# Loading the context in runs of 32 columns and turning it with VectorE's 32 by 32 block transposes

## What is computed

```
# reference, cut
x = first_block(...)          # mixers, gates, "mixed @ w_out", then an MLP: up, relu squared, down
hc = _modulate(_rmsnorm(ctx_2, norm_g), shift_c, scale_c)   # 256 x 2048
pc_kv = hc @ w_in_2[:, OFF_K:OFF_ZA]
kc = _rmsnorm(_heads(pc_kv, 0, 4), k_norm_g)
vc = _heads(pc_kv, KV_W, 4)
```

## Time and profile before

| | |
|---|---|
| median of 3 runs | 2193.26 us |
| the profiled execution, its own time | 2193.32 us |
| its span in the trace | 2191.5 us |
| TensorE busy (matmul) | 2180.9 us |
| TensorE weight load | 2050.2 us |
| VectorE busy | 1546.1 us (71%) |
| ScalarE busy | 1060.4 us (48%) |
| GpSimd busy | 103.1 us (5%) |
| DMA | 474.97 MB, mean 217 GB/s |

### The profile page before, as it was taken

How to read it: one execution, slowest core, us unless ns; L and a number is a source line. 1 busy time by engine, 2 the same in 40 slices (tenths; PEclk the granted TensorE clock), 3 DMA queues, 4 the chain that set the end, 5 groups by cost and what they waited for, 6 DMA issues and landing times.

```text
span 2191.5 us, 37576 instructions
## 1 busy us (share of the span) xinstructions
PE 2180.9 (100%) x15930; PEld 2050.2 (94%) x15930; DVE 1546.1 (71%) x1886; ACT 1060.4 (48%) x1382; POOL 103.1 (5%) x84
## 2 busy tenths in 40 slices
PE   9999999999999999999999999999999999999998
PEld 9999999999999889989988988998889999999987
DVE  7899588888889657544554555555768887776776
ACT  5444445544444546444543443444655555444443
POOL 1000000000000000000000000000101211110001
PEclk9999999999999999999999999999999999999999
DMA  8876676687787755656656656656755545678784
GB/s 276 245 242 199 199 252 223 227 279 259 253 282 263 240 183 182 194 192 193 195 194 194 194 194 196 200 191 204 246 172 164 165 136 178 220 269 285 257 276 158
DMA packets 248032, 474.97 MB, mean 217 GB/s; under 512 B 21526, under 2 KB 26000, under 8 KB 247096
## 3 DMA queue, kind: packets, MB, share of 16 engines
q1 hardware_dynamic: 243032, 454.40, 64.9%
q0 software_dynamic: 4832, 18.16, 2.5%
HBM read 468.30 MB, written 5.78 MB: 216 GB/s over the span
## 4 chain that ended last, share of the span: by engine, by line
PE 98%; DVE 1%; issue 0%; ACT 0%; DMA 0%; SPq 0%; DVEq 0%; POOLq 0%; POOL 0%; ACTq 0%
PE ps L907 21%; PE ps L909 20%; PE ps L908 20%; PE ps L900 11%; PE ps L901 11%; PE ps L902 11%; PE ps L825 1%; PE ps L703 0%; PE ps L748 0%; DMA raw<-in_w_in 0%; PE ps L735 0%; PE ps L814 0%; PE ps L813 0%; PE ps L815 0%; DVE wloW L1298 0%
## 5 line engine op out<-in xcount | busy, mean ns | idle before, releaser
L907 PE MATMUL ps<-op0h,whiW 128*128 128x256 f32 x3376 | 936.9, 278 | 1.4 <-DVE wloW L1298 1.2
L909 PE MATMUL ps<-op0h,wloW 128*128 128x256 f32 x3376 | 932.3, 276 | 0.0
L908 PE MATMUL ps<-op0l,whiW 128*128 128x256 f32 x3376 | 932.2, 276 | 0.0
L1298 DVE TENSOR_TENSOR wloW<-raw,whiW 128x1024 fp32r<-128x1024 f32 (+1 forms) x503 | 618.2, 1241 | 312.3 <-ACT whiW L954 310.3
L954 ACT ACTIVATE whiW<-raw 128x1024 fp32r<-128x1024 f32 (+1 forms) x504 | 529.7, 1059 | 574.6 <-PE ps L909 469.2
L907 PEld LDWEIGHTS ps<-op0h,whiW 128*128 128x128 f32 x3376 | 633.8, 188 | 4.0 <-DVE wloW L1298 2.1
L908 PEld LDWEIGHTS ps<-op0l,whiW 128*128 128x128 f32 x3376 | 633.9, 188 | 0.6
L909 PEld LDWEIGHTS ps<-op0h,wloW 128*128 128x128 f32 x3376 | 633.8, 188 | 0.0
L1298 DVE TENSOR_TENSOR wloT<-raw,whiT 128x1024 fp32r<-128x1024 f32 (+1 forms) x264 | 318.9, 1218 | 236.2 <-ACT whiT L954 235.0
L954 ACT ACTIVATE whiT<-raw 128x1024 fp32r<-128x1024 f32 (+1 forms) x264 | 273.9, 1048 | 286.2 <-PE ps L902 246.4
L900 PE MATMUL ps<-whiT,op1h 128*128 128x512 f32 x640 | 249.2, 389 | 0.0
(11 more groups left out here) (310 smaller groups left out, 2088.4 us busy)
## 6 DMA issues: line engine op xcount, KB each, us to landing
raw<-in_w_in SPq DMA_DIRECT2D x256, 512.0 KB, 4.3
raw<-in_w_up SPq DMA_DIRECT2D x128, 512.0 KB, 3.8
raw<-in_w_down SPq DMA_DIRECT2D x128, 512.0 KB, 4.0
raw<-in_w_ada SPq DMA_DIRECT2D x96, 512.0 KB, 4.5
raw<-in_w_gate SPq DMA_DIRECT2D x96, 512.0 KB, 5.0
raw<-in_w_out SPq DMA_DIRECT2D x64, 512.0 KB, 4.8
raw<-in_w_branch SPq DMA_DIRECT2D x48, 512.0 KB, 5.0
raw<-in_w_proj_a SPq DMA_DIRECT2D x24, 512.0 KB, 5.0
```

Source lines behind the costliest of these rows:

```text
L907: pe.matmul(o, wh, xh[:, ka, :], start=first and m % 2 == 0, stop=False, skip_group_check=True)
L908: pe.matmul(o, wh, xl[:, ka, :], start=False, stop=False, skip_group_check=True)
L909: mm = pe.matmul(o, wl, xh[:, ka, :], start=False, stop=last, skip_group_check=True)
L1298: v.tensor_tensor(wlo[job.mode][q % NSPL][:, :, 0:job.n], x, h.bitcast(F32), ALU.subtract).then_inc(s_lo, 1)
```

## The change

The context is loaded in another layout, and the turn from tokens on partitions to channels on partitions is done by VectorE.

- The load: 32 DMAs of 64 KB on GpSimd's queue instead of 4 of 512 KB, all behind one wait for the end of `g23` and all counted on one semaphore (512). Each brings 32 tokens (b) of 32 of every 128 channels (g) to 32 partitions: 16 runs of 32 columns, 128 bytes each, per partition. Partition 32g + r then holds token 32b + r, channels 128k + 32g to 128k + 32g + 31.
- The sums: `ctx_square` now stands in steps 272 and 273 and is four activations each, one for a group of 32 tokens, into eight columns. The sum of one token is spread over four partitions, so TensorE adds them in step 274 with a new part `ctx_sums`, one product of `foldm` with the eight columns. VectorE's `ctx_var` (step 275) adds eps to all eight, GpSimd takes the power once instead of twice, and `ctx_norm` (steps 276 and 277) is four instructions of 128x512 each.
- The turn: `ctx_turn(i)`, i = 0 to 7, on VectorE in step 278 + i is one transpose of 128x512 in 32 by 32 blocks from `ctxs` to `ctxt`, both on SBUF. The 32 products with the identity are gone from TensorE. ScalarE's `turn_x` for the unit stands in the same step 278 + i and reads `ctxt`, VectorE's stands in step 279 + i, ahead of `ctx_turn(i + 1)` in the table.

```diff
@@ -225,10 +225,9 @@
         for tt in range(2):
-            q = of["wo0"].first + 3 + 2 * tt
+            q = of["wo2"].first + tt
             side(act_at, q, "ctx_square", tt)
-            side(dve_at, q, "row_var", 1, tt)
-            side(dve_at, q + 1, "row_norm", 1, tt)
+            side(dve_at, q + 4, "ctx_norm", tt)
             q = of["wo3"].end + 1 + tt
@@ -239,7 +238,14 @@
             side(dve_at, q + 1, "row_norm", 3, tt)
-        for s, q0, n in ((1, of["wo0"].first + 9, 1), (2, of["kc"].first + 6, 2), (3, of["vc"].first + 7, 2)):
+        side(pe_at, of["wo2"].first + 2, "ctx_sums")
+        side(dve_at, of["wo2"].first + 3, "ctx_var")
+        for i in range(8):
+            q = of["wo2"].first + 6 + i
+            side(dve_at, q, "ctx_turn", i)
+            side(act_at, q, "turn_x", 8 + i)
+            side(dve_at, q + 1, "turn_x", 8 + i)
+        for s, q0, n in ((2, of["kc"].first + 6, 2), (3, of["vc"].first + 7, 2)):
             for i in range(8):
...
@@ -370,8 +376,8 @@
         g1b = bg("g1b", [128, 2048], 0)
-        ctxs = at("ctxs", [128, 2, 2048], op0_at)
-        ctxj = at("ctxj", [128, 2048], op0_at + 16384)
+        ctxs = at("ctxs", [128, 16, 8, 32], op0_at)
+        ctxt = at("ctxt", [128, 16, 256], op0_at + 16384)
         zs = bg("zs", [128, 16, 256], 8)
...
@@ -478,7 +484,7 @@
-            w = 4 if name in QK else 1
+            w = 8 if name == "ctx" else 4 if name in QK else 1
             c = col(f"n_{name}{tt}", 2 * w)
@@ -592,12 +598,12 @@
                 pool.dma_start(X[:, t, c:c + 1024], a["x"][0, 128 * t:128 * t + 128, c:c + 1024]).then_inc(s_xr, 16)
-            for i in range(4):
-                t, c = i // 2, 1024 * (i % 2)
-                pool.wait_ge(s_pe, of["g23"].end + 2 * i)
-                pool.dma_start(ctxs[:, t, c:c + 1024], a["ctx_2"][0, 128 * t:128 * t + 128, c:c + 1024]).then_inc(s_ctxin[t], 16)
+            ctx_parts = a["ctx_2"][0].rearrange("(b r) (k g c) -> g b r k c", r=32, g=4, c=32)
+            pool.wait_ge(s_pe, of["g23"].end)
+            for g in range(4):
+                for b in range(8):
+                    pool.dma_start(ctxs[32 * g:32 * g + 32, :, b, :], ctx_parts[g, b]).then_inc(s_ctxin, 16)
             rstd("ctx", 0)
-            rstd("ctx", 1)
             rstd("mixed", 0)
@@ -685,15 +691,12 @@
                     return
-                src = (None, ctxs, macc, macc)[s]
+                src = macc
                 ps = bank[4 + u % 4]
...
                     pe.wait_ge(s_turned, u - 11)
-                elif kp == 0 and s == 1:
-                    pe.wait_ge(s_ya, 8)
-                    pe.wait_ge(s_acol, 1)
                 elif s == 2:
@@ -712,6 +715,11 @@
                 pe.matmul(bank[4][0:8, 0:384], a5[0:32, 0:8], oneh[0:32, :], start=True, stop=True).then_inc(s_erow, 1)
+
+            def ctx_sums():
+                pe.wait_ge(s_sumsq, 4)
+                pe.wait_ge(s_ya, 8)
+                pe.matmul(bank[5][:, 0:8], foldm[:, :], norm_col("ctx", 0)[0], start=True, stop=True).then_inc(s_ctxsum, 1)
...
@@ -957,10 +965,11 @@
             def ctx_square(tt):
-                act.wait_ge(s_ctxin[tt], 32)
-                if tt:
-                    act.wait_ge(s_sumsq, 3)
-                square(ctxs, ctxj[:, :], "ctx", tt)
+                act.wait_ge(s_ctxin, 512)
+                for b in range(4 * tt, 4 * tt + 4):
+                    junk = ctxt[:, 2 * b:2 * b + 2, :].rearrange("p k (b c) -> p (k b) c", c=32)
+                    op = act.activation(junk, ctxs[:, :, b, :], ACT.Square, accum_out=norm_col("ctx", 0)[0][:, b:b + 1])
+                op.then_inc(s_sumsq, 1)
@@ -981,6 +990,8 @@
                 ps, tm = bank[4 + u % 4], tmp[2 + u % 2]
+                if s == 1:
+                    ps = ctxt[:, 2 * kp:2 * kp + 2, :].rearrange("p k t -> p (k t)")
                 act.wait_ge(s_turn, u - 7)
@@ -1333,6 +1344,24 @@
+            def ctx_var():
+                ss, rs = norm_col("ctx", 0)
+                v.wait_ge(s_ctxsum, 1)
+                v.tensor_scalar(rs, bank[5][:, 0:8], 1.0 / D, EPS, ALU.mult, ALU.add).then_inc(s_var, 1)
+
+            def ctx_norm(tt):
+                v.wait_ge(s_rstd, norm_no["ctx", 0])
+                for b in range(4 * tt, 4 * tt + 4):
+                    x = ctxs[:, :, b, :]
+                    op = v.tensor_scalar(x, x, norm_col("ctx", 0)[1][:, b:b + 1], None, ALU.mult)
+                op.then_inc(s_rows, 1)
+
+            def ctx_turn(i):
+                k = slice(2 * i, 2 * i + 2)
+                if i == 0:
+                    v.wait_ge(s_rows, 2)
+                v.transpose(ctxt[:, k, :].rearrange("p k t -> p (k t)"), ctxs[:, k, :, :].rearrange("p k b c -> p (k b c)")).then_inc(s_turn, 1)
+
             def row_var(s, tt):
```

More of the change, by code:

```diff
@@ L330, in program @@
         gqk = sb("gqk", [128, 2, 128])
-        mhalf = sb("mhalf", [128, 4])
+        mhalf = sb("mhalf", [128, 8])
         recip = sb("recip", [128, 16])
@@ L448, in program @@
         s_brm, s_mixv, s_mixh, s_mix = sem("branch_summed"), sem("mix_value"), sem("mix_high"), sem("mix_operand")
-        s_ctxin, s_xr, s_g1b = [sem("ctx_rows0"), sem("ctx_rows1")], sem("x_again"), sem("g1b")
+        s_ctxin, s_ctxsum, s_xr, s_g1b = sem("ctx_rows"), sem("ctx_sums"), sem("x_again"), sem("g1b")
         s_wosq, s_x1 = sem("wout_square"), sem("x1_rows")
@@ L468, in program @@
         s_out = [sem(f"out{i}") for i in range(5)]
-        norms = [("x0", 0), ("x0", 1), ("ctx", 0), ("ctx", 1), ("mixed", 0), ("mixed", 1), ("x1", 0), ("x1", 1), ("kc", 0), ("kc", 1),
+        norms = [("x0", 0), ("x0", 1), ("ctx", 0), ("mixed", 0), ("mixed", 1), ("x1", 0), ("x1", 1), ("kc", 0), ("kc", 1),
                  ("mlp", 0), ("mlp", 1), ("x2", 0), ("x2", 1), ("k", 0), ("k", 1), ("qq0", 0), ("qq0", 1), ("qq1", 0), ("qq1", 1),
@@ L847, in fourier_d @@
                 mm.then_inc(s_fd, 1)
-            parts = {"turn_x": turn_x, "vectors_b": vectors_b, "bias_row": bias_row, "ada_fold": ada_fold, "index_dots": index_dots, "pool_weight": pool_weight,
+            parts = {"turn_x": turn_x, "vectors_b": vectors_b, "bias_row": bias_row, "ctx_sums": ctx_sums, "ada_fold": ada_fold, "index_dots": index_dots, "pool_weight": pool_weight,
                      "scores1": scores1, "turn1": turn1, "values1": values1, "turn_x": turn_x,
@@ L1638, in _ @@
                      "softmax1_max": softmax1_max, "softmax1_scale": softmax1_scale, "values1": values1, "fold_map": fold_map, "ada_quarters": ada_quarters,
-                     "ada_columns": ada_columns, "row_var": row_var, "row_norm": row_norm, "turn_x": turn_x, "x1_add": x1_add, "mlp_add": mlp_add,
+                     "ada_columns": ada_columns, "ctx_var": ctx_var, "ctx_norm": ctx_norm, "ctx_turn": ctx_turn, "row_var": row_var, "row_norm": row_norm, "turn_x": turn_x, "x1_add": x1_add, "mlp_add": mlp_add,
                      "turn_qk": turn_qk, "split_kc": split_kc, "rotate": rotate, "softmax2_max": softmax2_max, "softmax2_less": softmax2_less, "softmax2_sum": softmax2_sum,
```

## The result

The changed kernel takes 2208.38 us, the median of 6 runs (2207.72 to 2209.63); the kernel before took 2193.27 us beside it (6 runs, 2193.2 to 2193.96). The ratio is 1.0069, 95% interval [1.0059, 1.008]: 15 us slower. The profiled execution took 2208.33 us, its span 2206.5 us, 15.0 more than the span before.

What follows compares the result with a forecast made beforehand. TensorE, busy end to end and 98% of the chain that ended last, was taken to bound the kernel. The sum was 2193.3 - 3.5 + 2.0 + 12.8 + 1.9 = 2206.5 us, 0.6% slower, range 2201.5 to 2215.

Steps and rivals of the forecast that it cites:

- 1 identity products gone: TensorE's 32 products with the identity, two blocks of 16 at 1.75 us each, go: gain 3.50 us.
- 6 the load: The 32 small context loads on GpSimd's queue land 20 us and more before ScalarE wants them: no cost.
- 2 `ctx_sums`: TensorE waits 1.65 us for ScalarE's squares before `ctx_sums`, plus 0.35 for product and refilled pipeline: loss 2.0 us.
- 4 the rounds: Steps 278 to 285: ScalarE and VectorE wait for each other, 5.01 us a round against 2.72: loss 12.8 us.
- 5 after chunk 288: VectorE's backlog delays `x1_add`, making chunks 291 to 293 late: loss 1.9 us, between 0 and 4.
- The loop: Steps 278 to 285: ScalarE's and VectorE's parts form one circle of 5.01 us a round, costing 12.8 us.
- The wait at `ctx_sums`: TensorE, before `ctx_sums` in step 274, waits 1.65 us for both halves of ScalarE's squares; loss 2.0 us in all.
- rival C: TensorE's clock falls in the rounds, a chunk lasting 5.44 us: 5 to 8 us more, 2212 to 2215; chance 0.08.
- rival A: GpSimd's loads go one at a time, the last landing 43 us after ScalarE wants it: about 2250 us; chance 0.07.
- part 6: The context load: landing 737 to 752, wanted at 772, weights landing some microseconds later harmless; cost taken as nothing.
- Step 5: After chunk 288: `x1_add` starts some 5.5 us after it, chunks 291 to 293 come late: loss 1.9 us.
- Rival B: In steps 278 to 285 VectorE's and ScalarE's work overlaps, rounds costing nothing: 2191.8 us, within 0.2%; chance 0.08.

Runs made afterwards that it cites:

- e1: The changed kernel with ScalarE's and VectorE's `turn_x` of the context one step later: 2194.57 us, ratio 1.0004 to the kernel before.
- e3: The changed kernel with only the context's squares moved four steps earlier, to steps 268 and 269: 2205.57 us, ratio 1.0056 to the kernel before.
- e6: The changed kernel with one more block transpose of 128x512 ahead of each of the eight, into an unread PSUM bank: 2213.85 us, ratio 1.0094.
- e7: The changed kernel with four products on idle data put before each of chunks 284 to 288 on TensorE: 2209.84 us, ratio 1.0074.
- e5: The changed kernel with VectorE's block transpose of the next unit ahead of the cast and subtraction of the last: 2201.05 us, ratio 1.0042.
- e9: e1 with four products of 256 columns on idle data ahead of TensorE's wait in `ctx_sums`: 2193.00 us, ratio 1.0001 to the kernel before.
- e4: The kernel before with 32 loads in small runs into the old layout, the context's parts eight steps later: 2193.94 us, ratio 1.0003.
- e8: e2 with the 32 loads in four groups of eight, at the ends of chunks 252, 255, 258 and 261: 2190.84 us, ratio 0.9989.
- e2: e1 with the context's squares also moved from steps 272 and 273 to 268 and 269: 2191.03 us, ratio 0.9991 to the kernel before.

## Why the prediction was right, step by step

The start times on TensorE's timeline give each term apart. The distance to the first of x1's identity products (833.85 before, 848.31 after) is 14.46 us:

| Step | predicted | measured in the trace | from |
|---|---|---|---|
| 1 identity products gone | -3.50 | -3.49 | chunk 272 starts 3.32 us earlier (770.66 against 773.98), with 0.17 lost at 748 |
| 6 the load | 0 | +0.17 | gap before 748.81 |
| 2 `ctx_sums` | +2.0 | +2.16 | 775.87 to 778.26, less the 0.23 of a matmul |
| 4 the rounds | +12.8 | +13.2 | chunk 274 at 778.26 to 288 at 829.57, less 14 x 2.722 |
| 5 after chunk 288 | +1.9 | +2.39 | 18.74 against 16.35 us to x1's products |
| sum | +13.2 | +14.4 | |

Another 0.5 us lies behind it, in one place: at 1991.29 TensorE stands 0.55 us behind the matmul before it, where 0.11 is usual, because ScalarE had waited 4.4 us for raw weights of `w_in`. The kernel before, e1 and e3 have no such wait of TensorE there, and in three experiments with the same rounds (e3, e6, e7) the time behind x1's products is as long as before. So it belongs to this execution and not to the change. Every term of the forecast came out within 0.5 us, so the total is not luck. No miss took time off, and so 13.2 us were forecast and 15 measured.

**The loop** was the deciding step, and it held in each of its parts: 5.01 us forecast, 5.02 measured. Inside it two sizes were off and cancelled: ScalarE's two activations take 1.00 from SBUF where the earlier trace rows had 0.91 from PSUM, and the transpose with its hand-over 0.74 where 0.80 was assumed; from SBUF to SBUF it lasts 0.70, next to the row's 0.72. e1 (order alone changed, the rounds gone), e5 (one part taken out of the circle, 1.06 less per round) and e6 (one part doubled, 0.59 more per round) show the mechanism itself, not only its sum. The 0.4 us beyond the forecast is mainly lead: `ctx_norm` took 1.6 us a step where 1.45 was assumed, the first transpose started 18.4 us after chunk 272 instead of 18.0, and the lead at chunk 281 was 4.2 us instead of 4.4. (In its range, the terms of the low end add up to -5.2 and not to the -5.0 written; nothing hangs on it.)

**The wait at `ctx_sums`** was right in kind and size (1.76 us idle, 2.16 in all), but a consequence was missed: the clock. The prediction looked for a falling clock in the rounds only (rival C), and had a clock below 1.00 there as a sign of being wrong. That sign came, 0.89, and the price that C put on it, 5 to 8 us, did not. C took whole chunks at half rate, 5.44 us; in the trace the last 7 matmuls of chunk 285 and the last 6 of chunk 287 ran at half rate, these chunks took 4.3 and 4.2 us, and that fits into a round of 5.02. The fall costs behind `ctx_sums`, 1.6 us in part of the executions, as e1, e9 and e7 show. For the changed kernel itself it is argued, not shown: its six runs stand in pairs at 2207.7, 2208.4 and 2209.6, the highest 1.9 above the lowest. The profiled one, 2208.33, is of the middle pair and had no such fall; the 0.5 us lost at 1991 are most of its distance to the lowest.

**The load** was forecast at nothing with 20 us of cover for its landing. The cover was real, if 15 us: rival A fell. The price is another one, on the weights beside it, and the sentence of part 6 that a weight landing some microseconds later costs nothing did not hold in every execution. ScalarE waited 11.3 us for `in_w_out` weights, five times, where it had waited for none; the lead of nearly three chunks took up all but 0.17 us in this execution, and all but 1.0 us in e4. The DMA queues of the two kernels show why. Before, 716 to 745 us, and after, 716 to 770 us (packets, MB, share of 16 engines):

```profile
q0 software_dynamic: 576, 2.10, 20.4%
```

```profile
q0 software_dynamic: 1024, 2.10, 25.0%
```

20.4% of 29 us is 5.9 us of all engines, 25.0% of 54 us is 13.5: the packets of the same 2.1 MB took 2.3 times the engine time. It is not a price of the pieces alone: with the same pieces in four groups (e8) it is 21.3% of 54 us, 11.5 us or 1.9 times. The page "DMA: Bandwidth & Descriptors" of the Trainium skill, section "Why small descriptors are slow (HBM only)", led to an estimate of 1.75; these traces agree with the direction and have 1.9 to 2.3.

**Step 5** was 0.5 us short. Chunks 291, 292 and 293 lost 1.2, 0.7 and 0.3 us, where 0.85, 0.7 and 0.35 were forecast, so the miss is before chunk 291: the prediction let `x1_add` start 5.5 us after chunk 288, it started 5.75 after (835.32). **Rival B** fell: the copies stood 5.02 us apart. e1 shows what the same work does in another order.

## What to carry to other kernels

When a part moves from TensorE to a helper engine, write down, for one step of the written order, who waits for whom, and add up the closed circle: engines that hand work to each other and back inside one step don't run side by side, and the sum of their parts, not the larger, is the step's length. One step between producer and consumer opened the circle here and was worth 13.8 us, more than the 3.5 us that the moved work cost on TensorE. Then the larger part counts: VectorE's 2.79 us a step beside TensorE's 2.72 leaves no room for more. A wait newly put in front of a busy TensorE costs its length and, in some executions here, 1.6 us of clock behind it. A load of small runs has its price on the loads beside it, so look there too; that pacing it makes the kernel faster is not shown here.

## What the runs showed of the hardware that was not expected

- A gap of 1.76 us on TensorE in otherwise full activity was followed in the traces of e1 and e7 by some 3 us at half rate (0.43 us between matmuls of 512 columns instead of 0.23), and in those of the changed kernel, e5 and e6 not. e1's 11 runs fall into 8 and 3, 1.7 us apart, with mean granted clocks of 0.998 and 0.999. Products on idle data in the gap made the median 1.6 us faster.
- In the rounds, gaps of 2 us every 5 us left the granted clock at 0.89 over 32 us, with half rate in two of the chunks only, and the time of the rounds as at 1.00 (25.19 us both).
- GpSimd issued 31 loads of 64 KB in runs of 128 bytes 0.65 us apart and then paused 10.4 us before the next; e2 shows the same pause, 9.0 us, and so does e8, 8.4 us, again before the 32nd although its loads were paced. e4 has loads of the same size and number of runs to other places and issued all 32 without a pause. What GpSimd waits for is not in the trace.
- The packets of 2.1 MB in runs of 128 bytes took 2.3 times the DMA engine time of the same bytes in runs of 4 KB, and 1.9 times when paced (e8).
- GpSimd's power takes 1.68 us on 8 columns, where 4 columns take 1.02. The number of columns is not all of it: on one column the changed kernel has instructions of 1.46 and 1.59 us too.
